# A decoder step in fp32 on one core: the work ahead of the experts is put in another order, with the whole value projection ahead of the output projection

## The reference

```
hn     = rmsnorm(h)                                   # 264 x 1024
z, xbc, dt, b, c, v, ga, gb = split(hn @ w_in)        # 64 blocks of 128 columns, and 16 for dt
xbc    = silu(conv4(xbc));  xs, B, C = split(xbc)
y      = ssd(xs, softplus(dt), -exp(a_log), B, C)     # prompt: 2 chunks of 128, 16 heads, 4 groups
                                                      # sample: s = exp(dt a) s + dt x B;  y = s C   (8 states of 1024 x 128)
y_a    = group_rmsnorm((y + d_skip xs) * silu(z))
y_b    = b * conv3(c * v)
h      = h + (sigmoid(ga) y_a + sigmoid(gb) y_b) @ w_out
k, v   = rmsnorm(mem) @ w_xk, rmsnorm(mem) @ w_xv     # 256 memory rows; the samples have caches of their own
h      = h + softmax(rmsnorm(h) @ w_xq . k / 16) . v @ w_xo
h      = h + moe(rmsnorm(h))                          # 32 experts, top 4, 25 MB of weights for each pair of experts
y      = rmsnorm(h)
```

## Time and profile before

| | us |
|---|---|
| median of 3 runs (lowest, highest) | 1551.15 (1549.5, 1552.83) |
| profiled execution, device time | 1553.77 |
| its span, first to last instruction | 1551.6 |
| TensorE busy in the span | 1462.9 |
| VectorE, ScalarE, GpSimd busy | 449.6, 216.3, 26.1 |
| mean granted TensorE clock | 0.968 |
| HBM traffic in the span | 490 MB, 316 GB/s on average |

### The profile page before, as it was taken

How to read it: one execution, slowest core, us unless ns; L and a number is a source line. 1 busy time by engine, 2 the same in 40 slices (tenths; PEclk the granted TensorE clock), 3 DMA queues, 4 the chain that set the end, 5 groups by cost and what they waited for, 6 DMA issues and landing times.

```text
span 1551.6 us, 16659 instructions
## 1 busy us (share of the span) xinstructions
PE 1462.9 (94%) x6505; PEld 745.5 (48%) x6505; DVE 449.6 (29%) x891; ACT 216.3 (14%) x392; POOL 26.1 (2%) x42
## 2 busy tenths in 40 slices
PE   7999999988598799999999999999999999999997
PEld 5888888665377583333333333333333333333332
DVE  2630030486613423222222222212213213213213
ACT  2111311311112221101101101001001001001002
POOL 0000000012000000000000000000000000000000
PEclk8999999989699888999999999999999999999999
DMA  5634443337124683999999999999999999999993
GB/s 156 248 131 145 162 161 121 115 118 248 68 109 152 253 356 120 399 430 429 427 429 427 429 429 428 428 428 428 429 429 427 429 428 428 430 427 429 429 428 152
DMA packets 68776, 490.31 MB, mean 316 GB/s; under 512 B 8483, under 2 KB 9915, under 8 KB 44157
## 3 DMA queue, kind: packets, MB, share of 16 engines
q1 hardware_dynamic: 65372, 478.61, 75.0%
q0 software_dynamic: 3184, 11.31, 2.2%
q10 hardware_dynamic: 196, 0.07, 0.0%
HBM read 481.94 MB, written 8.19 MB: 316 GB/s over the span
## 4 chain that ended last, share of the span: by engine, by line
PE 70%; DMA 21%; DVE 6%; issue 2%; SPq 1%; ACT 1%; DVEq 0%; ACTq 0%
PE bank L1124 65%; DMA ring<-in_w_gate_up 18%; PE bank L1133 4%; DMA projT<-in_state_ssm 2%; DVE projT L942 2%; DMA out<-projT 1%; SPq L386 0%; DVE conv L901 0%; DVE projT L831 0%; DVE projT L879 0%; DVE projT L883 0%; DVE projT L881 0%; DMA flat<-in_x_sample 0%; DVE xnT L704 0%; DVE projT L854 0%
## 5 line engine op out<-in xcount | busy, mean ns | idle before, releaser
L1124 PE MATMUL bank<-ring,projT 128*64 128x512 f32 (+1 forms) x2112 | 461.2, 596 | 20.4 <-DMA ring<-in_w_gate_up 19.9
L1124 PEld LDWEIGHTS bank<-ring,projT 128*64 128x64 f32 (+1 forms) x2112 | 149.7, 136 | 315.4 <-issue 312.8
L1124 PE MATMUL bank<-xnT,ring 128*128 128x264 f32 x1152 | 258.5, 388 | 3.1 <-DVE xnT L704 3.1
L1124 PEld LDWEIGHTS bank<-xnT,ring 128*128 128x128 f32 x1152 | 219.8, 191 | 41.4 <-issue 3.5
L1124 PE MATMUL bank<-flat,projT 128*64 128x512 f32 (+1 forms) x552 | 236.6, 582 | 0.0
L1124 PE MATMUL bank<-conv,projT 128*64 128x512 f32 x512 | 225.8, 594 | 0.0
L1124 PE MATMUL bank<-projT 128*128 128x512 f32 (+1 forms) x472 | 210.0, 584 | 8.3 <-DVE flat L846 2.4
L457 ACT ACTIVATE projT<-bank 128x512 f32<-128x512 f32 (+3 forms) x189 | 93.7, 515 | 559.5 <-PE bank L1124 556.5
L1124 PEld LDWEIGHTS bank<-flat,projT 128*64 128x64 f32 (+1 forms) x552 | 77.6, 143 | 139.4 <-issue 137.6
L1124 PEld LDWEIGHTS bank<-projT 128*128 128x128 f32 (+1 forms) x472 | 63.5, 169 | 152.6 <-issue 103.5
L1085 DVE TENSOR_SCALAR projT<-bank 128x512 f32<-128x512 f32 x32 | 20.6, 686 | 343.9 <-PE bank L1124 343.9
(11 more groups left out here) (234 smaller groups left out, 814.4 us busy)
## 6 DMA issues: line engine op xcount, KB each, us to landing
ring<-in_w_gate_up SPq DMA_DIRECT2D x96, 2048.0 KB, 16.2
ring<-in_w_down SPq DMA_DIRECT2D x32, 2048.0 KB, 13.1
ring<-in_w_in SPq DMA_DIRECT2D x16, 2048.0 KB, 11.0
flat<-in_w_gate_up SPq DMA_DIRECT2D x16, 2048.0 KB, 14.0
conv<-in_w_gate_up SPq DMA_DIRECT2D x16, 2048.0 KB, 18.4
flat<-in_w_down SPq DMA_DIRECT2D x16, 2048.0 KB, 15.8
conv<-in_w_down SPq DMA_DIRECT2D x16, 2048.0 KB, 20.2
ring<-in_cache_mem_k SPq DMA_DIRECT2D x4, 2048.0 KB, 7.7
```

The source lines that it names most:

```text
L1124: last[0] = pe.matmul(out, lhsT, rhs, start=start, stop=stop)
```

## The change

The expert loop and all behind it stay. Ahead of it:

- **Start.** The sums of squares of x are taken by VectorE from the rows as they arrive (`mean_squares`), the square root works on one number for each token, and a product with the identity (`rbc`) spreads it. SyncE issues x, then the first `w_in` chunk, then the small transfers between the chunks (`early`). dt is projected with the features on 16 partitions, in 16 instructions in place of 48. The memory rows are turned and normalised in between the first blocks.
- **Projections** in the order xbc (`xb`), c and v (`cc`, `cv`), b and z (`cb`, `z`), ga with `kp`, gb. The turns of xs and B stand among `cc` and `cv`, the SSD steps among `cb` and `z` (`STEP_AT`). The products with v and b read the bank directly.
- **Sample states.** Four buffers in place of two. B and C are turned once, written to HBM as 8 rows of 4 KB (`brow`, `rows_hbm`), and GpSimd loads each row back, spread over 128 partitions, two samples ahead (`bcr`). TensorE's 64 `bcs` products go. TensorE meanwhile does `ga`, `kp` and `gb`; then `gn` among the last four `gb`.
- **`vp`**, all four, behind `kT` and ahead of `wo`.
- **Second norm.** ScalarE writes the gained, unnormalised `xnT` as each `wo` block lands, so `q` starts at once, and the norm is multiplied in when VectorE empties `q`.
- **Attention** is laid among `q`: `qb` jobs go by half of the heads, 8 for the first half as soon as its blocks are there.
- **Ring.** `K0`, `K1`, `V2`, `V3` go to two further slots (`flat`, `conv`), `K2`, `K3` take the slots of `wo`; the first expert chunks are issued behind `so` 1, `so` 3 and `xo`.
- Loops over blocks on three engines are written out.

```diff
+PLAN = [("xT", 8, A_), ("par0", 1, A_), ("rbc", 1, D_), ("xb", 2, A_), ("dt", 1, D_), ("xb", 2, A_), ("memT", 2, A_),
...
+STEP_AT = {("cb", 2): 0, ("cb", 3): 1, ("cb", 5): 2, ("cb", 7): 3, ("z", 0): 4, ("z", 2): 5, ("z", 3): 6,
+           ("z", 5): 7, ("z", 6): 8, ("z", 7): 9}
...
+for _j in range(4):
+    PLAN += [("ga", 2, A_), ("kp", 1, A_)]
+for _j in range(8):
+    PLAN += [("gb", 1, A_)]
+    if _j >= 4:
+        PLAN += [("gn", 1, A_)]
+PLAN += [("kT", 4, A_), ("vp", 4, A_), ("wo", 8, D_), ("q", 2, D_), ("h1ss", 1, A_), ("q", 3, D_), ("att", 1, A_),
+         ("qb", 2, D_), ("q", 1, D_), ("att", 1, A_), ("qb", 2, D_), ("q", 1, D_), ("qb", 2, D_), ("q", 1, D_),
+         ("qb", 2, D_), ("pT", 2, A_), ("att", 2, A_), ("qb", 2, D_), ("o", 1, A_), ("qb", 2, D_),
+         ("qb", 2, D_), ("o", 1, A_), ("qb", 2, D_), ("sT", 1, D_), ("pT", 2, A_), ("o", 2, A_),
...
+            ("ga0", w_in(6160), 0, ("filled", "cb", 3)), ("kp0", wcols(a["w_xk"], 0), 1, ("filled", "cb", 7)),
+            ("ga1", w_in(6672), 2, ("filled", "z", 3)), ("kp1", wcols(a["w_xk"], 512), 3, ("filled", "z", 7)),
+            ("gb0", w_in(7184), 0, ("filled", "ga", 3)), ("gb1", w_in(7696), 1, ("filled", "kp", 1)),
+            ("vp0", wcols(a["w_xv"], 0), 2, ("filled", "ga", 7)), ("vp1", wcols(a["w_xv"], 512), 3, ("filled", "kp", 3)),
+            ("wo0", wcols(a["w_out"], 0), 0, ("filled", "gb", 3)), ("wo1", wcols(a["w_out"], 512), 1, ("filled", "gb", 7)),
+            ("K0", cache("cache_mem_k", 0), 4, ("flat_free",)), ("K1", cache("cache_mem_k", 1), 5, ("conv_free",)),
...
+            ("V2", cache("cache_mem_v", 2), 4, ("emptied", "qb", 9)), ("V3", cache("cache_mem_v", 3), 5, ("emptied", "qb", 11)),
+            ("xo0", wcols(a["w_xo"], 0), 0, ("emptied", "qb", 13)), ("xo1", wcols(a["w_xo"], 512), 1, ("emptied", "qb", 15))]
...
+            pool.dma_start(rows_hbm[:, :], brow).then_inc(S["rows_kept"], 16)
+            pool.wait_ge(S["rows_kept"], 16)
+            rows_load(0)
+            rows_load(1)
+            for b in range(TS):
+                pool.wait_ge(S["state_read"], b + 1)
+                if b + 2 < TS:
+                    rows_load(b + 2)
+                pool.dma_start(sout[b], sst[b % 4]).then_inc(state_out[b % 4], 16)
+                if b >= 1 and b + 3 < TS:
+                    pool.wait_ge(state_out[(b - 1) % 4], 16)
+                    state_load(b + 3)
...
             for i in range(TS):
-                s_ = sst[:, i % 2]
-                v.wait_ge(state_in[i % 2], 16 * (i // 2 + 1))
+                s_ = sst[i % 4]
+                v.wait_ge(state_in[i % 4], 16 * (i // 4 + 1))
                 st(v.tensor_tensor(out=s_, in0=s_, in1=bc(dec[:, :, i], P), op=ALU.mult))
-                b = filled(v, "bcs", 2 * i)
-                done(v.tensor_tensor(out=by_group(prod), in0=rows_of(b), in1=by_group(bc(dtx[:, :, i], P)), op=ALU.mult))
-                emptied(v, "bcs", 2 * i)
+                v.wait_ge(bcr_in[i % 2], 16 * (i // 2 + 1))
+                rows = [bcr[i % 2][:, j].unsqueeze(2).to_broadcast([P, G, 2, P]) for j in range(2)]
+                st(v.tensor_tensor(out=by_group(prod), in0=rows[0], in1=by_group(bc(dtx[:, :, i], P)), op=ALU.mult))
...
+            s.wait_ge(S["gated"], KB)
             for k in range(4):
+                gate_b(k)
             for k in range(KB):
+                square_group(k)
+            for k in range(4):
+                gate_b(4 + k)
+                b = filled(s, "gn", k)
+                done(s.activation(rgrp[:, k, :], b[:, 0:T], ACT.Sqrt, bias=eps[:, 0:1], scale=1.0 / 256), "gn", k)
```

More of the change, by code:

```diff
@@ L65 @@
[L65 to L73, removed]
@@ new lines, in _ @@
+            dtk, dta = dtm[:, 0:2], dtm[:, 2:4]
+            emptied(v, "par1")
+            scale_rows("mbc", mnT, mnT, NM, NMEM, "mem_normed")
+            for k in range(7, 12):
+                convolve(k)
+            b = filled(v, "acum")
+            done(v.tensor_copy(small[:, 0:64], b[:, 0:64]), "acum")
+            emptied(v, "acum")
+            st(v.tensor_tensor(out=small[:, 64:80], in0=small[:, 32:48], in1=small[:, 0:16], op=ALU.subtract))
+            st(v.tensor_tensor(out=small[:, 80:96], in0=small[:, 64:80], in1=small[:, 48:64], op=ALU.add))
@@ L759, in _ @@
+            v.tensor_tensor(out=small[:, 96:112], in0=small[:, 48:64], in1=small[:, 16:32],
+                            op=ALU.subtract).then_inc(S["acum_read"], 1)
+            for k in range(12, XB):
+                convolve(k)
             emptied(v, "mst")
@@ new lines, in add_to_h, with add_square @@
+            def add_to_h(name, k):
+                b = filled(v, name, k)
+                done(v.tensor_tensor(out=hT[:, k, :], in0=b[:, 0:T], in1=hT[:, k, :], op=ALU.add), name, k)
+            def add_square(k, sq, count):
+                v.wait_ge(S["h_squared"], count + k + 1)
+                return v.tensor_tensor(out=rinv[:], in0=rinv[:] if k > 1 else sq[:, 0, :], in1=sq[:, k, :], op=ALU.add)
+            for k in range(KB):
+                add_to_h("wo", k)
+                if k >= 2:
+                    st(add_square(k - 1, sqh, 0))
@@ new lines, in _ @@
+            for k in range(5):
+                scale_q(k)
+            att_max(0)
+            sample_scores(0)
+            sample_scores(1)
+            scale_q(5)
+            att_max(1)
+            sample_scores(2)
+            sample_scores(3)
+            scale_q(6)
+            probabilities(0)
+            sample_scores(4)
+            sample_scores(5)
+            scale_q(7)
+            sample_scores(6)
+            sample_scores(7)
+            att_max(2)
+            att_max(3)
+            sample_scores(8)
@@ L1135, in _ @@
             pe.wait_ge(S["consts_set"], 2)
-            pe.wait_ge(x_in, 32)
+            for t in range(3):
+                pe.wait_ge(x_in[t], 16)
             for k in range(KB):
@@ new lines, in _ @@
+            xb(0, 1)
+            pe.wait_ge(wdt_in, 16)
+            b = free_bank(pe, "dt")
+            for k in range(KB):
+                mm(b[0:H, 0:T], wdt[:, k, :], xnT[:, k, :], k == 0, k == KB - 1)
+            close("dt")
+            xb(2, 3)
+            pe.wait_ge(mem_in, 32)
+            mem_turns(0, 1)
+            xb(4)
+            mem_turns(2, 3)
+            xb(5)
+            pe.wait_ge(par1_in, 16 * 3)
+            b = free_bank(pe, "par1")
+            turn(b[:, 0:24], stage[0:24, 1, :])
```

1412 lines of the change are left out of this document (793 added, 619 removed).

## The result

The changed kernel takes 1467.72 us (median of 4 executions, 1465.85 to 1468.79). The ratio to the kernel before on the same chip is 0.9461, with a 95% interval of 0.9442 to 0.948: faster by 5.4%. One more execution of the kernel before, at 1718.09 us, was in a slow state and is in none of these numbers. On another chip the changed kernel took 1461.94 us (median of 6), ratio 0.9432 (0.9408 to 0.9456). I had predicted 1472, in a range from 1458 to 1500. The profiled execution took 1465.85 us with a span of 1463.6, where the sum of the prediction came to 1473.1.

The account below looks back on a forecast made before the run. TensorE's queue of blocks was to bound nearly everything ahead of an unchanged expert loop; its terms put the loop's start at 520.4 us for 598.9, 78.5 us off the 1551.15 median, say 1472 us, range 1458 to 1500.

Parts of the forecast that it names:

- first block: Start: TensorE's first projection block at 16.5 us, where it began at 40.62; 20 us kept for the range.
- b, z with the SSD: Projections of b and z with SSD steps among them: 79.1 us on TensorE, the steps' waits hidden under the blocks.
- `q` to `so`: Attention, from `q`'s start to `so`: 70 us, VectorE setting the pace, against 78.1 us before.
- to the loop: Stretch from `so` and `sx` to the expert loop: 57.7 us, as before, so the loop starts at 520.4 us.
- 32 small products of `dec`: Stage of `fin`, `dec`, `brow`: 32 small products at a turn's price each, 3.8 us.
- cold start: First blocks on TensorE at the lower clock: 3.5 us lost, taken at the upper end.
- low end of my range: 1458 us: small products and steps priced high by some 4 us, cold start by 3, attention by 7.
- rival (a): Sample states: spread rows landing late make TensorE wait at `gn` 0; 1482 to 1500 us, chance 0.17.
- 6 us of lateness: Sample states: transfers expected about 6 us late in all, under a slack of 9 us ahead of `gn` 0.
- The claim for the title's part: Gating and group norms beside `kT` and `vp`: 23.5 us of gating covered, with 17 us to spare ahead of `wo`.
- rival (b): First chunks late, attention no shorter, or banks held up: 8 to 20 us lost, 1482 to 1493 us, chance 0.10.
- rival (c): Sample states: VectorE's two-SBUF-operand operations and GpSimd's DMA issues shut each other out; 1473 to 1482 us, chance 0.04.

Follow-up runs that it names:

- experiment 5: Changed kernel with two buffers for the sample states in place of four: ratio 0.9628, median 1493.01 us.
- experiment 2: Changed kernel with `q` waiting again for the scaled `xnT` written by VectorE: ratio 0.9511, median 1470.42 us.
- experiment 8: Changed kernel with `pT` 2, 3 and `o` 2, 3 ahead of `sT` in place of behind it: ratio 0.9437, median 1460.92 us.
- experiment 3: Changed kernel with `vp` behind `wo` and `q` waiting for the scaled `xnT`, the norm's product behind the last `vp`: ratio 0.9533, median 1475.66 us.
- experiment 4: Changed kernel with `vp` behind `wo` and `q` waiting for the scaled `xnT`, the norm's product behind `vp` 1: ratio 0.9475, median 1469.32 us.

## Why the prediction was right

The mechanism was right: TensorE's queue of blocks bounds everything up to the attention, and the loop follows it. By its own steps, predicted and measured (in the profile of the changed kernel):

| step | predicted | measured |
|---|---|---|
| first block | 16.5 | 16.75 |
| xbc stage | 70.9 | 69.7 |
| c, v | 61.7 | 61.2 |
| b, z with the SSD | 79.1 | 76.6 |
| `fin`, `dec`, `brow` | 8.2 | 5.8 |
| `ga`, `kp`, `gb`, `gn` | 88.1 | 88.0 |
| `kT`, `vp` | 29.4 | 29.1 |
| `wo` | 28.5 | 28.6 |
| `q` to `so` | 70 | 69.3 |
| `so`, `sx` | 10.3 | 10.4 |
| to the loop | 57.7 | 57.2 |
| loop | 952.7 | 951.05 |

The span came out 9.5 us under the sum (1463.6 for 1473.1). Two terms of TensorE's work were mis-sized and make 4.9 of it. An SSD step's `bc` and `sc` take 1.21 us, and a double `y` 1.10, where I took the durations of single groups, which overlap: 8 x 1.21 + 4 x 0.59 + 4 x 1.10 = 16.4 us for 19.5 (the whole stage came out 2.5 less). And the 32 small products of `dec`, on 16 partitions, take 1.03 us, not a turn's price each (3.8). The cold start was 2.7 us (32 instructions in 9.88 us for 7.13), not 3.5. That the lower clock is its cause is read from durations alone, here and in the prediction: the profiles show a granted clock of 1.00 from their first us on. Of what the low end of my range named, the small products and steps gave what it had for them (some 4 us); the cold start gave 0.8 of 3 and the attention 0.7 of 7. The loop, 1.65 us shorter, is a difference that also lies between two profiles of the same stage in other runs (950.6 to 952.8).

The transfers were priced wrong, and that it didn't matter was in part luck. Rows, states and stores landed in 7.7 to 10 us, twice what a lone one took, and the write of the rows took 6.0 us for 2.8. A row's 9.0 us is beyond the 7.9 from which rival (a) makes the samples wait; its formula then gives (9.0 + 0.9 + 3.8)/2 = 6.85 us for 6.3 a sample, 4.4 us in all, and VectorE waited 3.7 us among the samples (13.7 us for rows altogether, but 10.6 of them ahead of the first). For `gn` 0 I had the squares at 301 us and 6 us of lateness, TensorE at 310.2, so 3 us to spare. Measured were 2.7, but from other terms: the first row was there at 241.7 us for 246, the lateness was 3.7 for 6, and TensorE came 6.3 us sooner. Had the rows landed only a little later, each us would have been one of the end, as experiment 5 shows for the same place. So the 0.17 that I gave that rival was not too much.

The claim for the title's part, that the gating is covered with 17 us to spare, was exact (17.5), though both its ends came some 7 us sooner than I had them (329.6 for 337, 347.1 for 353.9). What I missed is what a wait costs beyond its length: the slower clock behind it (experiments 2, 5 and 8). Of rival (b), the first chunks came in time, the attention did get shorter, and no bank held TensorE up. On rival (c), the lock, see the last section. In the last stage, which I carried over from before, the first gather varies by 5.5 us from run to run, more than any term of the sum was off.

The experiments take back the cover of the gating, the second norm, the order of the SSD steps and of the attention, and the buffers. None takes back the new start (first block at 16.75 us for 40.62), the projection of dt, the dropped `bcs` products or the new ring: their part of the 86 us is read from the two profiles, not shown by a run.

## What to carry to other kernels

When an engine is the bound, look for work without dependences (here `vp`) and lay it over the wait, but check that the first link of the hidden chain stands ahead of the cover: in experiment 3, with one product behind the cover in place of in its middle, the norm still cost 6.15 us (230.96 for 224.81), and in experiment 4 0.2 us. Price a wait of TensorE as its length plus what the lower clock costs behind it. That was 1.8 to 2.8 us here behind waits of 3.1, 4.7 and 27 us, nothing behind waits of up to 1.8 us, and up to 5.5 us at the gather, behind a wait of only 2.15. Fill waits that can't be removed with useful jobs first, with spare products second. Price transfers by their landing time in the company that they will have, not alone. Which part of the company slows them is not shown: the first spread row took 4.25 us while the core's DMA engines moved 215 GB/s.

## What the runs showed of the hardware

**The clock can stay low for a whole busy stretch.** Windows of the changed kernel over the first gather:

```profile
498.30:502.00 3.70, 3.70 (x5) 1.16 (x5) 2.88 (x15) 0.00 (x0) 0.00 (x0) 0.50 0.00 0
502.00:506.00 4.00, 4.00 (x6) 1.46 (x6) 0.00 (x0) 0.60 (x1) 0.00 (x0) 0.50 0.00 0
506.00:509.70 3.70, 3.70 (x6) 0.69 (x4) 0.00 (x0) 0.00 (x0) 0.00 (x0) 0.50 0.00 0
```

TensorE is busy throughout with products of 512 columns and stays at 1.2 GHz for 11 us. Before it lie 4.9 us with TensorE busy for 2.13. The Trainium skill, in the part cited with experiment 2, has the clock released once the array has been busy; in this stretch it was not, and the measurement decides. In the run with `vp` behind `wo`, the only one without spare products with a gather of 5.97 us, the clock never fell in the same wait (windows over the wait and the gather):

```profile
501.00:503.16 2.16, 0.01 (x1) 0.03 (x1) 1.93 (x8) 1.34 (x4) 0.83 (x1) 1.00 0.00 0
503.16:509.13 5.97, 5.97 (x13) 1.98 (x13) 2.88 (x15) 0.60 (x1) 0.00 (x0) 1.00 0.00 0
```

Why it fell in one run and not in another is open.

**GpSimd's copies hold VectorE up, its DMA issues don't.** In the run with the steps in a row, the router's scans on VectorE and GpSimd's copies into `acc` (timelines):

```profile
497.37 3.02 POOL L535 COPY projT<-projT 128x1024 f32<-128x1024 f32 x3 [35.44 <-ACT projT L545]
...
497.58 2.90 DVE L1203 TENSOR_TENSOR_SCAN projT<-projT 128x32 f32<-128x32 f32 x3
```

Three scans, 0.46 us otherwise, take 2.90 and end with the copies. In four profiles the copies start 0.2 us ahead of the scans, and in each the scans take 2.90 us and TensorE's wait for the ranks grows to as much as 4.0 us. They are the four in which TensorE's clock stays at 1.00 through the router; in the other nine it falls to 0.50 there for a few us, the turns of `hT` that the copies wait for take 4.3 to 5.2 us for 2.84, the copies start 0.9 to 1.4 us behind the scans, and that wait is under 1 us. So the faster clock loses time here: from the router's first product to the ranks the four take 11.8 us and the nine 9.3 to 11.2. In the changed kernel, one of the nine, one operation of two SBUF operands (L1212) takes 1.02 us for 0.26. But beside GpSimd's DMA issues VectorE keeps its pace (from the changed kernel):

```profile
253.05 1.23 DVE L1054 TENSOR_TENSOR flat<-flat,projT 128x1024 f32<-128x1024 f32 x1
254.31 1.23 DVE L1057 TENSOR_TENSOR projT<-projT 128x1024 f32<-128x1024 f32 x1
...
253.49 0.89 POOL L494 DMA_DIRECT2D projT<-in_state_ssm  x1
```

So rival (c) was wrong for issues, as the row of the kernel before had it (0.89 us each), and the Trainium skill, SBUF — State Buffer, section "Who interferes with whom", is borne out in two points: a VectorE instruction with two SBUF inputs is held up by a GpSimd instruction that reads SBUF, and descriptor writing, which the page only infers, is spared. That VectorE holds GpSimd up in the same way, no run here shows (the three copies took 2.99 to 3.03 us everywhere).
